# Two-layer trunk: gate and residual added ahead of the last out-projection, h of layer 1 shared by two engines, and steps moved to other slots

## The reference

```python
def reference(x, c, ...):
    cond = silu(c)
    for layer in range(2):
        mod = cond @ ada_w[layer] + ada_b[layer]           # 2048 -> 3 * 2048
        shift, scale, gate = jnp.split(mod, 3, axis=-1)
        h = rms_norm(x, norm_w[layer]) * (1.0 + scale) + shift
        y = moba_branch(h, ...) if layer == 0 else mlstm_branch(h, ...)
        x = x + gate * y
    return x
```

## Time and profile before

| | |
|---|---|
| median of 3 runs | 1549.04 us (1547.87 to 1555.16) |
| profiled execution | 1546.67 us, span 1544.9 us |
| PE busy | 1460.3 us, 95% |
| DVE busy | 1086.5 us, 70% |
| ACT busy | 745.7 us, 48% |
| TensorE clock granted, mean | 0.981 |
| granules of 12 matmuls, one after the other | 2.72 us each |

### The profile page before, as it was taken

How to read it: one execution, slowest core, us unless ns; L and a number is a source line. 1 busy time by engine, 2 the same in 40 slices (tenths; PEclk the granted TensorE clock), 3 DMA queues, 4 the chain that set the end, 5 groups by cost and what they waited for, 6 DMA issues and landing times.

```text
span 1544.9 us, 20188 instructions
## 1 busy us (share of the span) xinstructions
PE 1460.3 (95%) x7359; PEld 1233.7 (80%) x7359; DVE 1086.5 (70%) x1198; ACT 745.7 (48%) x1022; POOL 37.7 (2%) x79
## 2 busy tenths in 40 slices
PE   2789999899999996899999999999999999999998
PEld 2577778788788876789889889889889889889886
DVE  5898698978889875776766556556556556556557
ACT  3454456455544546544544554554544544444452
POOL 1000010000000000000000000000000000000000
PEclk9799999999999998999999999999999999999999
DMA  8999889878989764678856656656656666566563
GB/s 290 376 375 342 286 276 340 300 274 289 316 310 335 263 199 167 231 254 268 292 182 188 187 178 182 187 177 185 181 178 188 177 181 185 176 189 180 176 190 110
DMA packets 197391, 361.49 MB, mean 234 GB/s; under 512 B 13152, under 2 KB 47288, under 8 KB 197068
## 3 DMA queue, kind: packets, MB, share of 16 engines
q1 hardware_dynamic: 196272, 359.60, 71.6%
q10 hardware_dynamic: 1056, 1.06, 0.2%
HBM read 358.51 MB, written 2.11 MB: 233 GB/s over the span
## 4 chain that ended last, share of the span: by engine, by line
PE 80%; DVE 8%; DMA 4%; issue 4%; ACT 3%; SPq 1%; POOL 0%; DVEq 0%; ACTq 0%; POOLq 0%
PE proj L1216 24%; PE proj L1218 23%; PE proj L1217 23%; DVE ada_acc L782 3%; DMA raw<-in_att_w_in 2%; PE mix L1216 1%; PE mix L1218 1%; PE mix L1217 1%; ACT w_hi L507 1%; DMA ada_raw<-in_ada_w 1%; DVE w_lo L763 1%; PE mix L1450 1%; PE mix L1346 1%; PE mix L1413 1%; DVE stream L921 1%
## 5 line engine op out<-in xcount | busy, mean ns | idle before, releaser
L763 DVE TENSOR_TENSOR w_lo<-raw,w_hi 128x1024 fp32r<-128x1024 f32 x480 | 585.8, 1222 | 402.7 <-ACT w_hi L507 399.9
L507 ACT ACTIVATE w_hi<-raw 128x1024 fp32r<-128x1024 f32 x480 | 508.0, 1062 | 723.7 <-PE proj L1218 611.6
L1216 PE MATMUL proj<-w_hi,h_hi 128*128 128x512 f32 x1216 | 486.8, 400 | 8.3 <-issue 7.2
L1218 PE MATMUL proj<-w_hi,h_lo 128*128 128x512 f32 x1216 | 476.4, 392 | 0.0
L1217 PE MATMUL proj<-w_lo,h_hi 128*128 128x512 f32 x1216 | 476.3, 392 | 0.0
L1216 PEld LDWEIGHTS proj<-w_hi,h_hi 128*128 128x128 f32 x1216 | 230.1, 189 | 59.0 <-issue 10.8
L1217 PEld LDWEIGHTS proj<-w_lo,h_hi 128*128 128x128 f32 x1216 | 230.3, 189 | 49.8 <-issue 3.3
L1218 PEld LDWEIGHTS proj<-w_hi,h_lo 128*128 128x128 f32 x1216 | 229.8, 189 | 48.7
L782 DVE SCALAR_TENSOR_TENSOR ada_acc<-ada_raw,cond,ada_acc 128x1024 f32<-128x1024 f32 x180 | 229.8, 1277 | 3.2 <-DMA ada_raw<-in_ada_w 1.3
L1216 PE MATMUL proj<-h_hi,w_hi 128*128 128x256 f32 x512 | 146.4, 286 | 3.3 <-DVE h_lo L823 3.3
L1218 PE MATMUL proj<-h_hi,w_lo 128*128 128x256 f32 x512 | 145.6, 284 | 0.0
(11 more groups left out here) (196 smaller groups left out, 1090.9 us busy)
## 6 DMA issues: line engine op xcount, KB each, us to landing
raw<-in_mlstm_w_in SPq DMA_DIRECT2D x256, 512.0 KB, 3.7
ada_raw<-in_ada_w SPq DMA_DIRECT2D x192, 512.0 KB, 6.2
raw<-in_att_w_in SPq DMA_DIRECT2D x128, 512.0 KB, 7.4
raw<-in_mlstm_w_out SPq DMA_DIRECT2D x64, 512.0 KB, 4.2
raw<-in_att_w_out SPq DMA_DIRECT2D x32, 512.0 KB, 6.5
stream<-in_x SPq DMA_DIRECT2D x1, 2048.0 KB, 9.2
ada_raw<-in_x SPq DMA_DIRECT2D x4, 512.0 KB, 6.7
out<-stream SPq DMA_DIRECT2D x4, 512.0 KB, 2.8
```

Of the source, the lines that this page charges most:

```text
L507: act.activation(w_hi[:, c % LEAD, :], raw[:, c % LEAD, :], ACT.Copy).then_inc(hi_ready, 1)
L763: dve.tensor_tensor(w_lo[:, c % LEAD, :], raw[:, c % LEAD, :], w_hi[:, c % LEAD, :].bitcast(F32), ALU.subtract).then_inc(lo_ready, 1)
L1216: pe.matmul(out_, a_hi, b_hi, start=start, stop=False, **kw)
L1218: return pe.matmul(out_, a_lo, b_hi, start=False, stop=stop, **kw)
```

## The change

1. **Prologue.** All 8 copies to `xnT` are ACT's. `rope_tables` moves from ahead of take 13 to slot 38.
2. **Group 1 of layer 0** (`late0`). Its second rope moves from slot 72 to slot 73, behind `out_evac0` of chunk 0; its attention (`turn_qk0`, scores, softmax, `turn_p0`, `pv0`) comes 2 slots later, and so do `y0_out` (88 to 90) and the turn of y (90 to 92). The sums of layer 1's modulation at slots 86 and 96 move to 88 and 97. In a slot that has both, `out_evac0` now stands ahead of the other tasks of the groups.
3. **End of layer 0.** `x1_base(q)` multiplies the sum of groups 0 to 2 by the gate and adds x, for the four chunks at slots 150, 151, 152 and 154. The last out-projection's chunk is then multiplied by the gate out of PSUM and added (`layer0_end`). The loads of `w_lo` for the first granules of layer 1 are written out between these steps. The last of the eight squares is DVE's (`square_last`).
4. **h of layer 1, q = 5 and 7 and the other odd ones.** ACT makes `h_hi` only; DVE makes `h_full` itself from PSUM and the scales, in two operations, ahead of line 823.
5. **Head of layer 1.** The 16 gate takes of slots 0 to 26 now stand at slots 11 to 26, one in each, and `bc_mask` moves from slot 9 to slot 12. The other 16 are spread over 25 slots and not 27.

```diff
-        AT_GATE1 = ada_at(KT, 27)
+        AT_GATE1 = [{11 + a: [a] for a in range(KT)}, ada_at(KT, 25)]
...
+        def late0(g):
+            return 2 if g == 1 else 0
...
@@ norm_act @@
-                for t in range(NT):
+                for t in range(1 if layer and q == CHUNKS - 1 else NT):
...
@@ h_make @@
+                if layer and q % 2:
+                    op.then_inc(h_act, 1)
+                    continue
                 act.activation(h_full[:, q % 2, k * SEQ:(k + 1) * SEQ], src, ACT.Identity,
...
@@ h_rest @@
             dve.wait_ge(h_act, KT * layer + 2 * (q + 1))
+            if layer and q % 2:
+                for k in range(2):
+                    kt = 2 * q + k
+                    op = dve.tensor_scalar(h_full[:, 1, k * SEQ:(k + 1) * SEQ],
+                                           turn_bank(1, q)[:, k * SEQ:(k + 1) * SEQ],
+                                           scale_c[:, 1, kt:kt + 1], shift_c[:, 1, kt:kt + 1], ALU.mult, ALU.add)
...
-        def layer0_end(dve, q):
-            dve.wait_ge(out_evac, 2 + CHUNKS * (G0 - 1) + q + 1)
+        def x1_base(dve, q):
+            dve.wait_ge(out_evac, 2 + CHUNKS * (G0 - 2) + q + 1)
+            dve.wait_ge(gate_out, q + 1)
+            dve.wait_ge(x_again, 16 * CHUNKS)
             x_q = stream[:, :, q * NC:(q + 1) * NC]
             dve.tensor_tensor(x_q, x_q, gate_both(q), ALU.mult).then_inc(x1_step, 1)
             dve.wait_ge(x1_step, q + 1)
-            dve.tensor_tensor(x_q, x_q, ada_raw[:, q], ALU.add).then_inc(x1_chunk, 1)
+            dve.tensor_tensor(x_q, x_q, ada_raw[:, q], ALU.add).then_inc(x1_sum, 1)
+        def layer0_end(dve, q, c):
+            dve.wait_ge(granule_used, c + 1)
+            dve.wait_ge(x1_sum, q + 1)
+            last = ada_raw[:, q]
+            dve.tensor_tensor(last, pair0(O_, G0 - 1, 2 * q)[:], gate_both(q), ALU.mult).then_inc(out_evac, 1)
+            dve.wait_ge(out_evac, 2 + CHUNKS * (G0 - 1) + q + 1)
+            x_q = stream[:, :, q * NC:(q + 1) * NC]
+            dve.tensor_tensor(x_q, last, x_q, ALU.add).then_inc(x1_chunk, 1)
+        def square_last(dve):
...
@@ dve_program @@
-                if n == 13:
-                    rope_tables(dve)
-                    dve.wait_ge(rope_table, 1)
-                if n == 9:
-                    for q in range(4, UNIT):
-                        xnT_copy(dve, q)
...
-                {LAST0 - 1: [lambda: dve.wait_ge(gate_out, CHUNKS), lambda: dve.wait_ge(x_again, 16 * CHUNKS)]},
-                {LAST0 + 2 * q + 1: [lambda q=q: out_evac0(dve, G0 - 1, q, LAST0 + 2 * q + 1),
-                                     lambda q=q: layer0_end(dve, q)] for q in range(CHUNKS)})
-            run(dve, lo, 0, 0, NG0, layer0, -LEAD)
+                {i: [lambda q=q: x1_base(dve, q)] for q, i in enumerate((150, 151, 152, 154))})
+            run(dve, lo, 0, 0, NG0 - LEAD, layer0, -LEAD)
+            for q in range(1, CHUNKS):
+                layer0_end(dve, q - 1, LAST0 + 2 * q - 1)
+                lo(dve, 0, NG0 + q - 1)
+            layer0_end(dve, CHUNKS - 1, NG0 - 1)
+            square_last(dve)
             norm_sum(dve, 1)
+            lo(dve, 0, NG0 + CHUNKS - 1)
             norm_scale(dve, 1)
+            lo(dve, 0, NG0 + CHUNKS)
```

More of the change, by code:

```diff
@@ L483, in sp_program @@
                 load_in1(sp, 0, 0, NG0 + i, i)
-                for a in AT_GATE1.get(i - LEAD, []):
+                for a in AT_GATE1[0].get(i - LEAD, []):
                     if a == 0:
@@ L713, in act_program @@
             norm_act(act, 0)
-            for q in range(4):
+            for q in range(UNIT):
                 xnT_evac(act, q)
@@ L806, in norm_sum @@
         def norm_sum(dve, layer):
[L807 removed]
+            dve.wait_ge(xsq_ready, NT * CHUNKS * (layer + 1) - layer)
+            if layer:
+                dve.wait_ge(xsq_dve, 1)
             dve.tensor_reduce(xss, xsq, AX.X, ALU.add).then_inc(xss_ready, 1)
@@ L1112, in dve_program @@
                   for i, b in SUM_AFTER.items()],
-                {42: [lambda: rope(dve, 0, 0)], 45: [lambda: rope(dve, 0, 1)], 53: [lambda: max0(dve, 0)],
+                {38: [lambda: rope_tables(dve), lambda: dve.wait_ge(rope_table, 1)], 42: [lambda: rope(dve, 0, 0)], 45: [lambda: rope(dve, 0, 1)], 53: [lambda: max0(dve, 0)],
                  56: [lambda: inv0(dve, 0)], 63: [lambda: y0_out(dve, 0)], 65: [lambda: y_lo_dve(dve, 0)],
                  69: [lambda: gates_lo(dve)], 72: [lambda: dve.wait_ge(stream_zeroed, 1)]},
-                *[{GROUP0[g] + 8: [lambda g=g: rope(dve, g, 0)], GROUP0[g] + 16: [lambda g=g: rope(dve, g, 1)],
-                   GROUP0[g] + 22: [lambda g=g: max0(dve, g)], GROUP0[g] + 25: [lambda g=g: inv0(dve, g)],
-                   GROUP0[g] + 32: [lambda g=g: y0_out(dve, g)]} for g in range(1, G0)],
@@ L1119, in dve_program @@
-                {GROUP0[1] + 34: [lambda: y_lo_dve(dve, 1)], GROUP0[2] + 34: [lambda: y_lo_dve(dve, 2)],
+                {first + 2 * q + 1: [lambda o=o, q=q, first=first: out_evac0(dve, o, q, first + 2 * q + 1)]
+                 for o, first in enumerate(outs) for q in range(CHUNKS)},
+                *[{GROUP0[g] + 8: [lambda g=g: rope(dve, g, 0)],
+                   GROUP0[g] + 16 + late0(g) // 2: [lambda g=g: rope(dve, g, 1)],
+                   GROUP0[g] + late0(g) + 22: [lambda g=g: max0(dve, g)],
+                   GROUP0[g] + late0(g) + 25: [lambda g=g: inv0(dve, g)],
+                   GROUP0[g] + late0(g) + 32: [lambda g=g: y0_out(dve, g)]} for g in range(1, G0)],
```

62 lines of the change are left out of this document (32 added, 30 removed).

## The result

The changed kernel took 1554.85 us (median of 9 runs, 1553.32 to 1557.74), the kernel before 1550.8 (9 runs, 1547.87 to 1555.16). The ratio is 1.0032 with a 95% interval of 1.0021 to 1.0043: about 5 us slower (3 to 7), within the 0.5% that the forecast gave half of its chance, and inside its range. The two profiled executions differ by more, 8.2 us (spans 1553.1 and 1544.9): that of before, at 1546.67 us, was faster than all nine of its runs. Its lead lies ahead of granule 56.

A forecast was written before the change was run, and what follows sets the result against it. PE, busy 95% of the span, bounds the kernel, so only its waits and low-clock stretches can be won. Terms -3.0 - 0.8 + 4.1 + 9.8 - 0.8 - 5.5 = +3.8 us gave 1552.8 against the median 1549.04; range 1538 to 1562.

The forecast's parts named there:

- the prologue: Start to first modulation sum: 4.5 us less DVE work, 1.4 of it back as a tile wait; -3.0 us taken.
- The end of layer 0: Last out-projection: DVE stands for x and its queue delays two bank releases; +13.7 there, +9.8 us with the shorter tail.
- the second wait: End of layer 0, before granule 156: PE waits 4.5 us for DVE's queue to free a PSUM pair, plus 1.7 for clock.
- The tail: Behind the last granule of layer 0: DVE's scaling comes after 6.9 us instead of 10.8, so -3.9 us.
- Rival 1: All joins: they really get shorter, x and evacuations in time everywhere; -20 to -15 us, about 1531; chance 0.17.
- rival 2: End of layer 0: x lands earlier than read, giving -3 to +3 there, about 1543 us in all; chance 0.15.
- Group 1: Layer 0's group 1: rope behind an evacuation -0.8 us, attention 2 slots later +4.1 us.
- the wait at the modulation sum: Group 1's later attention: DVE's evacuation ends near 392, PE waits 2.0 us instead of 0.6, +1.4.
- The head of layer 1: Turn of the convolved k: wait of 6.25 us becomes 1.6, full clock behind it 0.9 more; -5.5 us.
- Rival 3: Layer 1 slots 11 to 26: dense takes bind DVE and DMAs, +8 us, so 1561; chance 0.18.
- My lower bound: Prologue: no gain, 0 us, if the DMAs set the first granule.
- h: h of layer 1: ACT drops one of four passes for odd q, shortening PE's waits on h_lo; -0.8 us.

The follow-up runs named there:

- e3: The kernel before with only the prologue change (8 copies on ACT, rope tables at slot 38): 1548.23 us, ratio 0.9989.
- e1: The changed kernel with SP loading x again four weight tiles earlier at the end of layer 0: 1548.75 us, ratio 0.9994.
- e5: The changed kernel with x loaded early and the last group's chunk 0 put ahead of the fourth gate and x on DVE: 1544.82 us, ratio 0.9963.
- e2: The changed kernel with the end of layer 0 put back as before, all other parts kept: 1545.71 us, ratio 0.9971.
- e6: The kernel of e5 with ACT squaring chunks 0 to 2 in slots 155, 157 and 158: 1541.24 us, ratio 0.9942.
- e12: The changed kernel with the first h and h_lo made ahead of a w_hi and a w_lo: 1556.89 us, ratio 1.004.
- e7: The kernel of e6 with group 1's second rope at slot 75 and group 2's first rope at slot 91: 1536.57 us, ratio 0.9923.
- e11: The changed kernel with ada tiles 16 to 47 loaded to half, 8.4 MB less, so their sums are not true: 1551.66 us, ratio 1.001.
- e9: The kernel before with only the h change (odd q of layer 1 shared by ACT and DVE): 1549.8 us, ratio 0.9997.
- e10: The kernel of e7 with the modulation sum before group 2 at slot 94, not 97: 1539.92 us, ratio 0.9934.
- e13: The kernel of e6 with group 1, its attention and the two modulation sums as before: 1538.64 us, ratio 0.9933.

## Why the prediction was right, and where it was not

**The sum was nearly right, and some of its terms were not.** Forecast +3.8 us, measured about +5 by the runs and +8.2 between the two profiled executions. The stages add up to +8.1. What the forecast lacked is 3.1 us in the prologue and 1.7 in granule 160. With e3's -1.7 in place of the +0.1 for the prologue the stages give +6.3, inside the 3 to 7 of the runs.

**The end of layer 0** carried the forecast: +13.7 forecast and +13.6 measured on granule 159. Both mechanisms were there as described, the DMA of x (e1) and the queue of gate and x ahead of the first bank release (e5), and e2 shows that nothing else is in it. Two small errors cancel inside: the second wait was 3.3 where I had 4.5 to 4.7, and granule 154 ran wholly at 0.50, its twelve matmuls in 5.3 us, 2.6 above the 2.72 where I had charged 1.7. The tail was 3.0 shorter, not 3.9. Here too an error hid another. The 3.5 that I took for sum, root and waits does not come out of my rows: from 583.46 + 1.2 to 587.35, less one square of 0.6, are 2.1, and so the tail should have read 5.4 us and not 6.9. Measured were 7.6 (DVE's scaling at 601.18, granule 159 at 593.56), since I had let the last two squares run side by side and had not seen that ACT's other six stood behind a w_hi. With those out of the way (e6) PE's wait is 2.1 shorter, which gives 5.5. Rival 1 and rival 2 fell with DVE's 6.38 us for x.

**Group 1** came out at +3.2 for +3.3, in part by luck. The wait moved from granule 76 to 78 (3.0 us for 3.4), and y0_out cost 2.66 for 2.7. The slow stretch behind the turn of y (0.64 from 365.2 to 370) cost 1.6, which I had left out of the value, and the wait at the modulation sum was 0.70 and not 2.0. The slow stretch made PE later there, but it does not explain the short wait: e1, e2, e5 and e12 had full clock behind the turn of y and waited 0.7 all the same. In e5 DVE's copy came 25.1 us after the turn of y began and here 26.7, so it moves with PE, and its 392 was not set by the amount of DVE's work alone. Even with the ropes moved further (e7), the stage came only back to the time that it has without part 2.

**The head of layer 1** gave 5.9 for 5.5. The clock stayed at full, so all of the 1.4 us came and not 0.9 of it. Rival 3 did not appear: granules 176 on take the same time to 0.01 us. The stretch from 60 to 77 of the earlier trace rows was the right precedent, the one from 111 to 128 was not. Its two waits, of 3.3 us and of 2.2, stand in e11 too, where the DMAs have less to move, so DMA load alone does not make them.

**The prologue is the term that was mis-sized**, at -3.0. I wrote that 4.5 us of DVE work less, less one tile time of 1.4, come to PE. But 3.4 us came back as waits of DVE for tiles (4.31 for 0.95), and the first sum began 1.2 us sooner, not 3. Of the 1.7 us at granule 0, 1.4 were left at granule 10 and nothing at granule 19. What the term is worth at the end is less sure: +0.1 in the pair of traces, -1.7 (-0.2 to -3.3) in e3's runs. That the DMAs take such a gain back is shown by e12, with weights that land every 2.7 us whenever the first granule starts, and supported by e11; they were at a share of 1.02 to 1.05 already in the earlier trace rows. My lower bound had this case, at the first granule; it belonged at granules 5 to 20.

**h** at -0.8: alone 0 (e9), and nothing in the changed kernel (10.65 us behind the wait, 10.51 before). I had looked for it in PE's waits on h_lo, and had left out the clock behind this join, which moved that part by 1.5 us down (e2) and 0.9 up (e5).

The Trainium skill, "TensorE: Matmul & The Clock Gate", section "HAM oscillation — how this bites in real kernels", describes waits that each throw the next matmuls back to the slow clock. For the two new waits at the end of layer 0 the traces agree: in the changed kernel, e1, e11 and e12 waits of 3.3 to 5.5 us were each followed by a slow stretch, worth 1.9 to 2.8 us. Of the 13.6 us the two waits are 8.7 and slow matmuls nearly all of the other 4.9; without them the term would have come out at 5.7 instead of 10.6. Elsewhere they agree only in part. The same wait of 2.66 us before the turn of y was followed by slow matmuls in three kernels (changed, e6, e11) and not in four (e1, e2, e5, e12); in e5:

```profile
366.20:371.00 4.80, 4.80 (x26) 4.09 (x27) 4.80 (x5) 1.91 (x2) 0.00 (x0) 1.00 0.83 282
```

Behind 1.7 us (before the turn of k) and 1.3 us (e5) the clock stayed at full.

Of the versions run, e7 is the fastest: 0.9923 (0.99 to 0.9945) of the time before, 12 us less. By the intervals e6, e10 and e13 cannot be told from it.

## What to carry to other kernels

Work that is moved forward out of a tail goes into a queue. Before moving it, list for each waiting engine which instruction frees what it waits for, and count everything that now stands ahead of that one, waits for DMAs included. Here 9.6 us of early gate and x delayed two bank releases and cost 13.6 to save 3. With the release put first and x loaded sooner the same idea broke even (e5: +2.2 and -2.1). A net gain of 3 us came with e6: 2.1 of it because ACT's squares no longer stood behind a w_hi that waits for the last granule, and 0.9 that e5's trace had lost to the slow clock.

A gain at the start of a stretch in which the DMAs are full can be gone by its end; here 3.1 us were gone after ten granules. Sum the bytes up to the next common point first.

A single pair of traces can mislead by some microseconds. Executions with the same prologue ended granule 55 up to 6.7 us apart, while the stage of granules 112 to 159 of kernels with the same end of layer 0 repeated to 0.2 us, and that from 176 on to 0.03. Stages show what a change did where the total does not.

## What the runs showed of the hardware

- Waits of PE in the middle of a steady stream did not have one price. Behind those of 3.9 to 5.5 us (granules 76, 154 and, in e1, 156) the next matmuls ran slow in every trace, 1.6 to 2.8 us extra. Behind one of 2.66 us, at the same place, the clock was 0.64 in the changed kernel and 1.00 in e5 and e12, and the granule took 8.07 or 6.49 us. Behind one of 3.3 us before granule 19 the kernel before kept its clock (0.99 from 111 to 128), and the changed kernel did not (0.89).
- Behind the same join the clock differed between kernels with the same work there (0.59 in e9, 1.00 in e2, 0.50 in e5), worth 1.5 us one way and 0.9 the other: a difference of this size in one trace shows nothing of the code.
- 16 slots with a weight tile and a gate tile of 512 KB each cost PE nothing in the head of layer 1: from 681 to 689 and from 689 to 697 the changed kernel's DMAs moved 387 and 398 GB/s, and PE was busy throughout.
